# The expert router fed from the rows ahead of LayerNorm, in column halves

## The chip, the cores and the metric

The kernel runs on one core of a Trainium2 chip. The metric is device time in microseconds (us), as the median of several runs. TensorE does the matrix products, VectorE and ScalarE work on rows and on what TensorE leaves in PSUM, GpSimd builds constants and issues the gathers, SyncE issues nearly all loads. In the profile they are PE (PEld for its weight loads), DVE, ACT, POOL and SP; a q behind the name (SPq) is the engine's own queue of DMA issues and waits.

## The reference, cut to what matters

One layer on 512 tokens of 1024 channels, float32. Retention and a gated recurrence are projected, merged and passed through an output projection; then

```python
x = _layer_norm(DEEPNORM_ALPHA * x + merged @ w_out, ln1_g, ln1_b)
# hierarchical MoE
g_logits = xt @ w_group + b_group                    # 4 groups, argmax
e_logits = xt @ w_exp_router + b_exp_router          # 32 experts, top 2 inside the chosen group
h = silu(xb @ w_e_gate[e]) * (xb @ w_e_up[e]);  y = h @ w_e_down[e]
x = _layer_norm(DEEPNORM_ALPHA * x + moe, ln2_g, ln2_b)
```

Each of the 32 experts has three matrices of 2 MB, so 192 MB of weights are read, whatever the tokens choose.

## The kernel before

**Stages.** Everything up to the output projection works on channels by tokens, with every float32 operand split in a high and a low part and three products for each (`products`, L1367 to L1369). The output projection (`project`, L1543) gives rows: tile t of 128 tokens and column half `half` go into PSUM bank t, 8 blocks k of three products each. The order on TensorE is written out by hand: half 0 of tiles 0 to 3, then half 1 of tiles 0 to 3.

**LayerNorm 1 and the router.** For each of the eight half tiles VectorE waits for `proj_ok`, forms z = alpha * x + projection in place in `x2` (L1161) and takes the half's statistics (`half_stats`, L1138). After the second half of a tile, `layer_norm` (L1140 to L1153) aggregates them, has ScalarE take the root (L758), and writes the normalised tile over z in `x2` (`x2_ok`). TensorE then turns the whole tile into banks 4 and 5 with eight transposes (`turn_x2`, L1527), ScalarE copies it to `x2_t` (`x2t_out`, L733) and stores the tile to memory (`x2_dram`, L736), and TensorE multiplies it with the 36 router columns (`router`, L1535) into bank 6. The calls between the projections are: after `project(1, 1)` `turn_x2(0)`; after `project(1, 2)` `router(0)`, `turn_x2(1)`; after `project(1, 3)` `router(1)`, `turn_x2(2)`; then `router(2)`, `turn_x2(3)`, `router(3)`. VectorE adds the bias to all four tiles' logits at once and runs the selection: a chain of some twenty small operations up to `members_ok`, ranks by TensorE (L1584), `hot_r`, the lists by TensorE (L1593, L1598) and the row numbers `first_x` (L1253). GpSimd, which builds its constants once `proj_ok` has reached eight (L493), waits for `first_x` and for the stored rows, and gathers the rows of expert 0 from `x2_dram` (L511). In its waits TensorE runs products of the identity whose result is not used (`keep_warm`, 12, 3 and 14 calls).

**The experts.** SyncE loads the weights in pieces of 1 MB through a ring of 21 places (`load_m`, L412). Some places overlie older data and have a wait of their own:

```python
if n == 9:  sp.wait_ge(proj_ok, TT)
if n == 13: sp.wait_ge(proj_ok, 2 * TT)
if n == 19: sp.wait_ge(x2_ok, TT)
if n == 20: sp.wait_ge(routed, TT)
if n >= MRING: sp.wait_ge(m_done, n + 1 - MRING)
```

Piece 21 thus waits until the first half of expert 0's gate and up products has been used. For each expert TensorE turns the gathered rows (`turn_x`, L1608), multiplies with gate and up in two halves (`gate_up`, L1618), with down (L1647), and puts the result back to its tokens (`combine`, L1671). LayerNorm 2 and the output follow the last expert.

Of the kernel before, what the change touches and what calls it, by code (L numbers as in the profile page):

```python
# [48 lines left out]
OVER = (BLOCKS - 1) * EXPERTS  # L49
NO_ROW = 4096  # L50
NEAR = 4

# [78 lines left out]
def layer(nc, io, out):  # L131
    ctx = ExitStack()
    with ctx:
# [50 lines left out]
        x2 = at("x2", 64, [P, TT, D])  # L184
        x2_t = at("x2_t", 192, [P, 2, D])
        ln1_b_in, ln2_g_in = at("ln1_b_in", 196, [P, D]), at("ln2_g_in", 48, [P, D])
# [52 lines left out]
        hot_g, hot_1, hot_2, e8 = rt("hot_g", 16), rt("hot_1", 32), rt("hot_2", 32), rt("e8", 32)  # L239
        slot_i, red, res = rt("slot_i", 32, I32), rt("red", 4), rt("res", 64)  # L240
        assert rt_kb[0] <= 204.25
        ids, ids_w = at("ids", 128, [P, 2 * TT, 32]), at("ids_w", 129, [P, 2 * TT, 32])
# [34 lines left out]
        proj_ok, z_ok, x2_var, x2_std, x2_ok = (sem(n) for n in ("proj_ok", "z_ok", "x2_var", "x2_std", "x2_ok"))  # L277
        x2_turned, x2t_ok, routed, x2_stored = sem("x2_turned"), sem("x2t_ok"), sem("routed"), sem("x2_stored")
        router_in, consts_ok = sem("router_in"), sem("consts_ok")
# [33 lines left out]
        def _(sp):  # L313
# [66 lines left out]
            w_rt_v = w_rt[:, :].rearrange("p (k n) -> p k n", k=KD)  # L380
            for a in range(KD // NEAR):
                ks, rows_a = slice(NEAR * a, NEAR * a + NEAR), slice(P * NEAR * a, P * NEAR * (a + 1))
                sp.dma_start(w_rt_v[:, ks, 0:GROUPS], io["w_group"][0][rows_a].rearrange("(p b) n -> p b n", b=NEAR)).then_inc(router_in, 16)
                sp.dma_start(w_rt_v[:, ks, GROUPS:36], io["w_exp_router"][0][rows_a].rearrange("(p b) n -> p b n", b=NEAR)).then_inc(router_in, 16)
            sp.dma_start(b_rt[:, 0:GROUPS], row(io["b_group"])).then_inc(router_in, 16)
            sp.dma_start(b_rt[:, GROUPS:36], row(io["b_exp_router"])).then_inc(router_in, 16)
            load_qk(0, Unit(U_QK0))
            with sp.Fori(0, HEADS - 1) as h:
# [154 lines left out]
        def _(act):  # L543
# [188 lines left out]

            def x2t_out(t):  # L733

                act.wait_ge(x2_ok, t + 1)
                act.dma_start(x2_dram[t * P:(t + 1) * P, :], x2[:, t, :]).then_inc(x2_stored, 16)  # L736
                act.wait_ge(x2_turned, t + 1)
                if t >= 2:
                    act.wait_ge(routed, t - 1)
                if t == 0:  # L740
                    act.wait_ge(qk_split, 4 * HEADS)
                copy(x2_t[:, t % 2, :].rearrange("p (b n) -> p b n", b=2), bank[:, 4:6, :]).then_inc(x2t_ok, 1)

            def order_rows(dst, given):
# [8 lines left out]

            for t in range(TT):
                if t:
                    x2t_out(t - 1)
                act.wait_ge(x2_var, t + 1)
                act.activation(scale_v[:, 0:1], mv[:, 1:2], ACT.Sqrt).then_inc(x2_std, 1)  # L758
            x2t_out(TT - 1)

# [67 lines left out]
        def _(dve):  # L828
# [304 lines left out]
            dve.wait_ge(res_in, 16)  # L1133
            dve.wait_ge(ln1_ordered, 1)

# [3 lines left out]

            def layer_norm(t, ln, mid, start, end, var, std, ok):  # L1140
# [5 lines left out]
                z, g = (v.rearrange("q (c n) -> q c n", c=2) for v in (x2[:, t, :], ln[:, 0, :]))  # L1146
                step(dve.scalar_tensor_tensor(mid, z, mv[:, 0:1], g, ALU.subtract, ALU.mult))  # L1147
                dve.wait_ge(std, t + 1)
                step(dve.reciprocal(scale_v[:, 1:2], scale_v[:, 0:1]))
                step.wait()  # L1150
                for c_ in range(2):
                    cols = slice(512 * c_, 512 * c_ + 512)
                    last = dve.scalar_tensor_tensor(end(x2[:, t, cols]), start(mid[:, c_, :]), scale_v[:, 1:2], end(ln[:, 1, cols]), ALU.mult, ALU.add)  # L1153
                last.then_inc(ok, 1)

            for half in range(2):
                for t in range(TT):
                    n = TT * half + t + 1
                    dve.wait_ge(proj_ok, n)
                    z = x2[:, t, 512 * half:512 * half + 512]  # L1160
                    dve.scalar_tensor_tensor(z, z, ALPHA, bank[:, t, :], ALU.mult, ALU.add).then_inc(z_ok, 1)  # L1161
                    dve.wait_ge(z_ok, n)
                    half_stats(t, half)
                    if half:
                        mid = bank[:, t - 1:t + 1, :] if t else bank[:, 6:8, :]
                        layer_norm(t, ln1, mid, by_rows, stored_rows, x2_var, x2_std, x2_ok)


            dve.wait_ge(router_in, 96)
            dve.wait_ge(consts_ok, 1)  # L1170
            dve.wait_ge(routed, TT)
            lg = logit[:, :].rearrange("p (t n) -> p t n", t=TT)
            step(tt(lg, bank[:, 6, 0:TT * 36].rearrange("p (t n) -> p t n", t=TT),
                    b_rt[:, :].unsqueeze(1).to_broadcast([P, TT, 36]), ALU.add))
            step.wait()

# [176 lines left out]
            for t in range(TT):  # L1353
                half_stats(t, 0)
                half_stats(t, 1)
                mid = bank[:, 0:2, :] if t % 2 == 0 else bank[:, 4:6, :]
                layer_norm(t, ln2, mid, lambda v: v.rearrange("q (b p) -> q p b", b=NEAR),
                           lambda v: v.rearrange("q (p b) -> q p b", b=NEAR), f_var, f_std, f_ok)
# [3 lines left out]
        def _(pe):  # L1362
# [163 lines left out]

            def turn_x2(t):  # L1527
                pe.wait_ge(x2_ok, t + 1)
                if t:
                    pe.wait_ge(x2t_ok, t)  # L1530
                for k in range(KD):
                    last = pe.transpose(bank[:, 4 + k // 4, P * (k % 4):P * (k % 4) + P], x2[:, t, P * k:P * k + P], ident[:, :])
                last.then_inc(x2_turned, 1)

            def router(t):  # L1535
                pe.wait_ge(x2t_ok, t + 1)
                pe.wait_ge(router_in, 96)
                for k in range(KD):
                    last = pe.matmul(bank[:, 6, 36 * t:36 * t + 36], x2_t[:, t % 2, P * k:P * k + P], w_rt[:, 36 * k:36 * k + 36],  # L1539
                                     start=k == 0, stop=k == KD - 1)  # L1540
                last.then_inc(routed, 1)
# [16 lines left out]
            for t in (0, 1):  # L1558
                project(0, t, range(6, KD))
            for t in (2, 3):  # L1560
                project(0, t, range(KD))
            pe.wait_ge(ret_out, 8 * HEADS + 8)
            for t in range(TT):
                pe.wait_ge(z_ok, t + 1)
                project(1, t, range(KD))
                if t:
                    if t >= 2:
                        router(t - 2)
                    turn_x2(t - 1)
            router(TT - 2)  # L1570
            turn_x2(TT - 1)
            router(TT - 1)

            def keep_warm(n):

                for _ in range(n):
                    pe.matmul(bank[:, 1, 0:P], ident[:, :], ident[:, :], start=True, stop=True)

            keep_warm(12)
            pe.wait_ge(members_ok, 1)  # L1580
# [188 lines left out]
```

## Time and profile before

| what | us |
|---|---|
| median of 3 runs (lowest, highest) | 1299.18 (1298.66, 1301.23) |
| the profiled execution's own time | 1297.71 |
| its span | 1295.7 |
| what lies around the span | 2.0 |
| busy in the span: PE, DVE, ACT, POOL | 1246.7, 656.3, 410.8, 63.7 |

All times of rows are counted from the start of the span. A share of 1.0 in the DMA column means that all 16 DMA engines are busy; PEclk is the clock granted to TensorE as a share of 2.4 GHz, so 0.50 is 1.2 GHz. Durations of single matmuls overlap; the chain of waits gives how long they take in sequence.

### The profile page before, as it was taken

The numbers are of one execution on the slowest core, as the hardware profiler recorded it, in microseconds if no ns is written. First come the engines' busy times: TensorE is split into PE (matmuls) and PEld (weight loads), VectorE is DVE, ScalarE is ACT, GpSimd is POOL, SyncE is SP. The second block draws the span as 40 slices with busy tenths as digits, with TensorE's granted clock in tenths as the row PEclk, the third lists the DMA queues.
The fourth block names the chain that finished last, engine by engine and source line by source line (L and its number), as shares of the span: only waits on it lengthen the run. The fifth ranks groups of instructions, "written<-read, shape, count | busy, mean of one in ns | idle before, by whom it ended". The sixth has DMA issues, their size and how long they took to land.

```text
span 1295.7 us, 16051 instructions
## 1 busy us (share of the span) xinstructions
PE 1246.7 (96%) x6122; PEld 844.2 (65%) x6122; DVE 656.3 (51%) x946; ACT 410.8 (32%) x572; POOL 63.7 (5%) x70
## 2 busy tenths in 40 slices
PE   7999999999999999999999998999999999999892
PEld 6888887887888888888888887343343343334331
DVE  5496666335447337437433855244444444444347
ACT  4766755222433333333343412111111111111111
POOL 1000000000000000000005201000000000000000
PEclk9999999999999999999999998999999999999997
DMA  8322222363323223222223399799999999999992
GB/s 248 87 84 81 83 82 73 85 171 96 99 66 98 81 81 94 82 77 86 81 76 103 102 406 426 311 416 408 418 415 415 413 415 420 411 416 418 411 413 83
DMA packets 141512, 286.11 MB, mean 221 GB/s; under 512 B 9984, under 2 KB 107376, under 8 KB 116880
## 3 DMA queue, kind: packets, MB, share of 16 engines
q1 hardware_dynamic: 137680, 276.81, 57.2%
q0 software_dynamic: 2624, 4.33, 1.0%
q10 hardware_dynamic: 1152, 4.19, 0.9%
q8 instruction: 38, 0.62, 0.2%
q14 instruction: 18, 0.15, 0.0%
HBM read 285.17 MB, written 4.33 MB: 223 GB/s over the span
## 4 chain that ended last, share of the span: by engine, by line
PE 88%; DMA 7%; DVE 2%; ACT 1%; issue 1%; ACTq 0%; SPq 0%; DVEq 0%; POOLq 0%
PE bank L1367 19%; PE bank L1368 19%; PE bank L1369 19%; PE bank L1618 15%; PE bank L1647 7%; DMA m_raw<-in_w_e_up_dram 6%; PE bank L1671 4%; PE bank L1640 1%; PE bank L1608 1%; PE bank L1539 1%; PE bank L1467 1%; DMA x_rows<-in_x_dram 1%; DVE x L1153 0%; DVE stats L1138 0%; DVE bank L1147 0%
## 5 line engine op out<-in xcount | busy, mean ns | idle before, releaser
L836 DVE TENSOR_TENSOR w_lo<-raw,w_hi 128x1024 fp32r<-128x1024 f32 x120 | 148.4, 1238 | 184.8 <-ACT w_hi L545 183.5
L1618 PE MATMUL bank<-m_raw,xe 128*64 128x512 f32 x1024 | 233.4, 598 | 7.8 <-DMA m_raw<-in_w_e_up_dram 7.0
L832 DVE TENSOR_TENSOR x<-x,bank 128x1024 f32<-128x1024 f32 x124 | 145.8, 1217 | 170.9 <-PE bank L1671 170.9
L1367 PE MATMUL bank<-xt_hi,w_hi 128*128 128x512 f32 x576 | 225.0, 391 | 2.5 <-ACT merge L634 1.0
L1369 PE MATMUL bank<-xt_hi,w_lo 128*128 128x512 f32 x576 | 224.2, 389 | 0.0
L1368 PE MATMUL bank<-xt_lo,w_hi 128*128 128x512 f32 x576 | 224.1, 389 | 0.0
L545 ACT ACTIVATE w_hi<-raw 128x1024 fp32r<-128x1024 f32 x120 | 126.2, 1057 | 172.2 <-PE bank L1369 172.1
L1618 PEld LDWEIGHTS bank<-m_raw,xe 128*64 128x64 f32 x1024 | 70.2, 136 | 133.5 <-issue 132.5
L1367 PEld LDWEIGHTS bank<-xt_hi,w_hi 128*128 128x128 f32 x576 | 108.1, 188 | 25.8 <-ACT merge L634 1.4
L1369 PEld LDWEIGHTS bank<-xt_hi,w_lo 128*128 128x128 f32 x576 | 108.1, 188 | 22.6
L1368 PEld LDWEIGHTS bank<-xt_lo,w_hi 128*128 128x128 f32 x576 | 108.2, 188 | 21.9
L1647 PE MATMUL bank<-m_raw,ht 128*64 128x512 f32 x496 | 113.3, 598 | 0.0
L545 ACT ACTIVATE gu_sb<-bank 128x512 f32<-128x512 f32 x32 | 19.1, 598 | 258.8 <-PE bank L1618 258.8
L1647 PEld LDWEIGHTS bank<-m_raw,ht 128*64 128x64 f32 x496 | 32.9, 136 | 55.3 <-issue 53.3
L1307 DVE SCALAR_TENSOR_TENSOR y_lo<-bank,first_w,y_hi 128x512 fp32r<-128x512 f32 x31 | 23.3, 751 | 84.2 <-ACT y_hi L791 84.2
L1671 PEld LDWEIGHTS bank<-y_hi,pick 64*128 64x128 f32 x248 | 23.2, 184 | 55.0 <-issue 48.7
L1671 PE MATMUL bank<-y_hi,pick 64*128 64x512 f32 x248 | 55.5, 444 | 2.0 <-DVE y_lo_last L1307 1.6
L791 ACT ACTIVATE y_hi<-bank,first_w 128x512 fp32r<-128x512 f32 x31 | 21.3, 687 | 93.1 <-PE bank L1647 93.1
L511 POOL DMA_INDIRECT xg<-x_dram,first_x x32 | 30.1, 939 | 412.4 <-PE bank L1608 392.9
L1367 PE MATMUL bank<-w_hi,xt_hi 128*128 128x512 f32 x128 | 49.8, 389 | 0.0
L1367 PE MATMUL bank<-ret_hi,w_hi 128*128 128x512 f32 x128 | 49.8, 389 | 0.0
L1368 PE MATMUL bank<-w_lo,xt_hi 128*128 128x512 f32 x128 | 49.8, 389 | 0.0
(252 smaller groups left out, 1675.2 us busy)
## 6 DMA issues: line engine op xcount, KB each, us to landing
m_raw<-in_w_e_gate_dram SPq DMA_DIRECT2D x64, 1024.0 KB, 27.1
m_raw<-in_w_e_up_dram SPq DMA_DIRECT2D x64, 1024.0 KB, 26.5
m_raw<-in_w_e_down_dram SPq DMA_DIRECT2D x64, 1024.0 KB, 27.4
raw<-in_w_in_dram SPq DMA_DIRECT2D x88, 512.0 KB, 3.9
raw<-in_w_ret_o_dram SPq DMA_DIRECT2D x16, 512.0 KB, 3.3
raw<-in_w_lru_o_dram SPq DMA_DIRECT2D x16, 384.0 KB, 3.3
raw<-in_w_out_dram SPq DMA_DIRECT2D x8, 512.0 KB, 3.5
x_rows<-in_x_dram ACTq DMA_DIRECT2D x4, 512.0 KB, 5.4
```

The source lines that it names most:

```text
L511: pool.indirect_dma_start(xg[0:ROWS, :], None, x2_dram, bass.IndirectOffsetOnAxis(ap=idx, axis=0), bounds_check=last_x, oob_is_err=False). ...
L545: return act.activation(dst, src, ACT.Copy)
L791: act.activation(stored_rows(dst[:, :]), by_rows(bank[:, b, :]), ACT.Identity, scale=w).then_inc(yhi_ok, 1)
L832: return dve.tensor_tensor(dst, a, b, op)
L836: return dve.tensor_tensor(dst, a, b_r.bitcast(F32), ALU.subtract)
L1307: dve.scalar_tensor_tensor(stored_rows(dst[:, :]), by_rows(bank[:, b, :]), w, stored_rows(high[:, :].bitcast(F32)), ALU.mult, ALU.subtract ...
L1367: pe.matmul(dst, sh, mh, start=first and x == 0, stop=False)
L1368: pe.matmul(dst, sh, ml, start=False, stop=False)
L1369: ins = pe.matmul(dst, sl, mh, start=False, stop=last and x == n - 1)
L1618: last = pe.matmul(bank[side:side + ROWS, 0, :], xe[:, 4 * half + k, :], w[:, FE * k:FE * k + FE], start=half == 0 and k == 0, stop=half = ...
L1647: last = pe.matmul(bank[ROWS * c_:ROWS * c_ + ROWS, b, :], h[:, 2 * half + k, :], w[:, D * k + 512 * c_:D * k + 512 * c_ + 512], start=hal ...
L1671: last = pe.matmul(bank[:, (2 if t % 2 == 0 else 6) + b, :], choose[side:side + ROWS, P * t:P * t + P], y[side:side + ROWS, :], start=x == ...
```

## The change

The router's input is no longer the normalised tile but z. With LayerNorm written out, x . w = rstd * (z . (g w) - mean * sum(g w)) + sum(b w), and the mean is folded in as well by taking each column's mean off g w. So the router matrix is scaled by `ln1_g` and centred once, and only the factor rstd of a row and a constant row are left for the end.

- **Fold.** `w_rt` is loaded with channel k * 128 + p on partition p in place k (two DMAs instead of four), and `ln1_g` and `ln1_b` as 16 rows `ln_rows` (two more DMAs). TensorE turns these rows once (before tile 2 of half 0), VectorE forms g w and b w and their sums over k (`fold_ln`, after its second half tile), TensorE sums over partitions with a matrix of ones (after half 0), VectorE finishes matrix and bias (`fold_totals`, after its fourth half tile).
- **Half tiles.** The unit of turning and routing is a half tile: four transposes into bank 4 or 5 (`turn_z`), one copy of 128 x 512 (`zt_out`), four products (`router`). They run in the order `TURNS`, and TensorE's calls are put inside the projections of half 1: after blocks 0 and 1, and after blocks 2 to 4; the router calls stand behind the projection.
- **Logits.** The halves of tiles 0 to 2 that were routed in half 0 are copied out of bank 6 once and added later (`logits`); tile 3 accumulates in bank 7. `layer_norm` writes over z only once the half tile has been turned.
- **Store.** `store_x2` is a step of its own in ScalarE's order. `keep_warm(12)` becomes `keep_warm(16)` and writes bank 5.

```diff
+TURNS = (0, 1, 2, 4, 3, 5, 6, 7)
                 if n == 20:
-                    sp.wait_ge(routed, TT)
+                    sp.wait_ge(routed, 2 * TT)
...
+            def zt_out(n):
+                act.wait_ge(z_turned, n + 1)
+                if n >= 4:
+                    act.wait_ge(routed, n - 3)
+                if n == 0:
+                    act.wait_ge(qk_split, 4 * HEADS)
+                if n == 2:
+                    act.wait_ge(ln1_ordered, 1)
+                copy(z_t[:, n % 4, :], bank[:, 4 + n % 2, :]).then_inc(zt_ok, 1)
...
+            for n in range(3):
+                zt_out(n)
+            root(0)
+            zt_out(3)
+            zt_out(4)
+            store_x2(0)
+            root(1)
+            zt_out(5)
+            store_x2(1)
+            root(2)
+            zt_out(6)
+            store_x2(2)
+            zt_out(7)
+            root(3)
+            store_x2(TT - 1)
...
+            def fold_ln():
+                dve.wait_ge(router_in, 96)
+                step(dve.memset(ones[:, :], 1.0))
+                dve.wait_ge(ln_turned, 1)
+                step(tt(wb3, w3, bank[:, 7, KD:2 * KD].unsqueeze(2).to_broadcast([P, KD, 36]), ALU.mult))
+                step.wait()
+                step(tt(w3, w3, bank[:, 7, 0:KD].unsqueeze(2).to_broadcast([P, KD, 36]), ALU.mult))
+                step(dve.tensor_reduce(w_sum[:, 36:72], wb3.rearrange("p k n -> p n k"), AX, ALU.add))
+                step.wait()
+                dve.tensor_reduce(w_sum[:, 0:36], w3.rearrange("p k n -> p n k"), AX, ALU.add).then_inc(w_summed, 1)
+            def fold_totals():
+                dve.wait_ge(w_totals, 1)
+                step(tt(b_rt[:, :], b_rt[:, :], bank[:, 7, 100:136], ALU.add))
+                dve.scalar_tensor_tensor(w3, bank[:, 7, 64:100].unsqueeze(1).to_broadcast([P, KD, 36]), -1.0 / D, w3,
+                                         ALU.mult, ALU.add).then_inc(w_folded, 1)
+            def logits(t):
+                dve.wait_ge(routed, TURNS.index(TT + t) + 1)
+                base = b_rt[:, :]
+                if t < TT - 1:
+                    step(dve.scalar_tensor_tensor(lg[:, t, :], lg[:, t, :], rstd[:, t:t + 1], base, ALU.mult, ALU.add))
+                    step.wait()
+                    base = lg[:, t, :]
+                dst = bank[:, 7, 0:36] if t == TT - 1 else bank[:, 6, 36 * t:36 * t + 36]
+                dve.scalar_tensor_tensor(lg[:, t, :], dst, rstd[:, t:t + 1], base, ALU.mult, ALU.add).then_inc(logits_ok, 1)
             for half in range(2):
                 for t in range(TT):
                     n = TT * half + t + 1
+                    if n == 2 * TT:
+                        logits(0)
+                        logits(1)
...
+                    if n == 2:
+                        fold_ln()
+                    if n == TT:
+                        fold_totals()
+                    if n == TT + 1:
+                        dve.wait_ge(routed, 3)
+                        dve.tensor_copy(lg[:, 0:3, :], bank[:, 6, 0:108].rearrange("p (t n) -> p t n", t=3)).then_inc(halves_read, 1)
...
+            logits(2)
+            logits(3)
...
             for t in range(TT):
                 pe.wait_ge(z_ok, t + 1)
-                project(1, t, range(KD))
-                if t:
-                    if t >= 2:
-                        router(t - 2)
-                    turn_x2(t - 1)
-            router(TT - 2)
-            turn_x2(TT - 1)
-            router(TT - 1)
+                project(1, t, range(2))
+                turn_z((0, 3, 5, 6)[t])
+                if t == 0:
+                    turn_z(1)
+                project(1, t, range(2, 5))
+                if t < 2:
+                    turn_z((2, 4)[t])
+                project(1, t, range(5, KD))
+                for n in ((0, 1, 2), (3,), (4, 5), (6,))[t]:
+                    router(n)
+            turn_z(7)
+            router(7)
```

## Rows read from the trace of the kernel before

**Rows 1.** Groups of waits, 750 to 1296 us: us in total, times, longest.
```profile
PE bank L1618 <- DMA m_raw<-in_w_e_up_dram: 7.0, 10, 1.3
```
**Rows 2.** Chain that ended last, in order of time: start, us, what.
```profile
777.85 1.71 PE bank L1539 x16
779.56 0.91 PE bank L1532 x8
...
808.68 3.63 DMA xg<-x_dram,first_x
...
813.81 7.09 PE bank L1618 x32
...
1223.82 26.22 DMA m_raw<-in_w_e_up_dram
```
**Rows 3.** Stretches: busy us (count) of each engine, clock, DMA share, GB/s.
```profile
808.00:812.00 4.00, 3.85 (x47) 3.62 (x43) 3.11 (x17) 0.00 (x0) 1.03 (x1) 1.00 0.67 273
812.00:816.00 4.00, 2.87 (x18) 1.35 (x20) 1.86 (x6) 0.60 (x1) 1.00 (x1) 1.00 0.15 41
816.00:820.00 4.00, 4.00 (x22) 1.43 (x20) 0.00 (x0) 0.00 (x0) 0.00 (x0) 1.00 0.38 102
...
1200.00:1220.00 20.00, 17.28 (x92) 7.10 (x90) 7.26 (x9) 3.12 (x6) 0.94 (x1) 1.00 1.02 408
```
**Rows 4.** VectorE in order of time: start, us, line, operation, shapes [idle before].
```profile
760.68 0.69 DVE L1161 SCALAR_TENSOR_TENSOR x<-x,bank 128x512 f32<-128x512 f32 x1 [1.18 <-PE bank L1369]
...
785.98 0.69 DVE L1161 SCALAR_TENSOR_TENSOR x<-x,bank 128x512 f32<-128x512 f32 x1 [2.72 <-PE bank L1369]
...
789.74 0.16 DVE L1149 RECIPROCAL scale_v<-scale_v 128x1 f32<-128x1 f32 x1 [0.71 <-ACT scale_v L758]
789.94 1.41 DVE L1153 SCALAR_TENSOR_TENSOR x<-bank,scale_v,ln 128x512 f32<-128x512 f32 x2
...
798.52 0.17 DVE L1185 TENSOR_REDUCE res<-logit 128x4 f32<-128x16 f32 x1
...
803.44 0.29 DVE L832 TENSOR_TENSOR mem_bf<-mem 128x128 bf16<-128x128 f32 x1
```
**Rows 5.** SyncE's queue, issues of weight pieces 12, 13 and 20 (with 21).
```profile
761.99 0.81 SPq L423 DMA_DIRECT2D m_raw<-in_w_e_gate_dram  x1
785.97 0.33 SPq L423 DMA_DIRECT2D m_raw<-in_w_e_up_dram  x1
...
798.07 19.75 SPq L423 DMA_DIRECT2D m_raw<-in_w_e_down_dram  x2
```
**Rows 6.** DMA issues of six short stretches (762, 786, 798, 818, 808, 844): us to landing.
```profile
m_raw<-in_w_e_gate_dram SPq DMA_DIRECT2D x1, 1024.0 KB, 29.0
...
m_raw<-in_w_e_up_dram SPq DMA_DIRECT2D x1, 1024.0 KB, 7.4
...
m_raw<-in_w_e_down_dram SPq DMA_DIRECT2D x1, 1024.0 KB, 13.9
...
m_raw<-in_w_e_down_dram SPq DMA_DIRECT2D x1, 1024.0 KB, 4.8
...
xg<-x_dram,first_x POOLq DMA_INDIRECT x1, 3.6
...
xg<-x_dram,first_x POOLq DMA_INDIRECT x1, 7.2
```
**Rows 7.** TensorE in order of time, around the granted clock's low stretch.
```profile
789.67 1.98 PE L1539 MATMUL bank<-w_rt,x_t 128*128 128x36 f32 x16 [1.11 <-ACT x_t L545]
...
794.41 3.63 PE L1539 MATMUL bank<-w_rt,x_t 128*128 128x36 f32 x16 [1.11 <-ACT x_t L545]
797.84 4.84 PE L1577 MATMUL bank<-ident 128*128 128x128 f32 x24
...
808.46 3.39 PE L1577 MATMUL bank<-ident 128*128 128x128 f32 x28
812.44 0.68 PE L1608 MATMUL bank<-ident,xg 64*128 64x64 f32 x8 [0.59 <-DMA xg<-x_dram,first_x]
```
**Rows 8.** Stretches as in Rows 3, where the granted clock fell.
```profile
791.60:792.30 0.70, 0.70 (x6) 0.70 (x5) 0.00 (x0) 0.00 (x0) 0.00 (x0) 0.52 1.08 456
```

More of the change, by code:

```diff
@@ L184, in layer @@
         x2 = at("x2", 64, [P, TT, D])
-        x2_t = at("x2_t", 192, [P, 2, D])
+        z_t = at("z_t", 192, [P, 4, D // 2])
+        w_b, ones, w_sum = at("w_b", 192, [P, KD * 36]), at("ones", 193.125, [P, P]), at("w_sum", 193.625, [P, 72])
         ln1_b_in, ln2_g_in = at("ln1_b_in", 196, [P, D]), at("ln2_g_in", 48, [P, D])
@@ L240, in layer @@
         slot_i, red, res = rt("slot_i", 32, I32), rt("red", 4), rt("res", 64)
+        ln_rows, rstd = rt("ln_rows", P), rt("rstd", TT)
         assert rt_kb[0] <= 204.25
@@ L380, in _ @@
             w_rt_v = w_rt[:, :].rearrange("p (k n) -> p k n", k=KD)
[L381 to L384, printed above, removed]
+            sp.dma_start(w_rt_v[:, :, 0:GROUPS], io["w_group"][0].rearrange("(k p) n -> p k n", p=P)).then_inc(router_in, 16)
+            sp.dma_start(w_rt_v[:, :, GROUPS:36], io["w_exp_router"][0].rearrange("(k p) n -> p k n", p=P)).then_inc(router_in, 16)
             sp.dma_start(b_rt[:, 0:GROUPS], row(io["b_group"])).then_inc(router_in, 16)
             sp.dma_start(b_rt[:, GROUPS:36], row(io["b_exp_router"])).then_inc(router_in, 16)
+            for r, name in ((0, "ln1_g"), (KD, "ln1_b")):
+                sp.dma_start(ln_rows[r:r + KD, :], io[name][0].rearrange("(k p) -> k p", p=P)).then_inc(router_in, 16)
             load_qk(0, Unit(U_QK0))
@@ L752, in _, with store_x2, root @@
             order_rows(ln1[:, 1, :], ln1_b_in).then_inc(ln1_ordered, 1)
-            for t in range(TT):
-                if t:
-                    x2t_out(t - 1)
+            def store_x2(t):
+                act.wait_ge(x2_ok, t + 1)
+                act.dma_start(x2_dram[t * P:(t + 1) * P, :], x2[:, t, :]).then_inc(x2_stored, 16)
+            def zt_out(n):
[7 more added lines that the diff above has]
+                copy(z_t[:, n % 4, :], bank[:, 4 + n % 2, :]).then_inc(zt_ok, 1)
+            def root(t):
                 act.wait_ge(x2_var, t + 1)
                 act.activation(scale_v[:, 0:1], mv[:, 1:2], ACT.Sqrt).then_inc(x2_std, 1)
-            x2t_out(TT - 1)
+            for n in range(3):
[13 more added lines that the diff above has]
+            store_x2(TT - 1)
             act.wait_ge(exp_ok, 1)
@@ L1133, in _, with layer_norm @@
             dve.wait_ge(res_in, 16)
-            dve.wait_ge(ln1_ordered, 1)
             def half_stats(t, half):
                 step(dve.bn_stats(stats[:, 12 * t + 6 * half:12 * t + 6 * half + 6], x2[:, t, 512 * half:512 * half + 512]))
-            def layer_norm(t, ln, mid, start, end, var, std, ok):
+            def layer_norm(t, ln, mid, start, end, var, std, ok, inv=scale_v[:, 1:2]):
                 step.wait()
@@ L1148, in layer_norm @@
                 dve.wait_ge(std, t + 1)
-                step(dve.reciprocal(scale_v[:, 1:2], scale_v[:, 0:1]))
+                step(dve.reciprocal(inv, scale_v[:, 0:1]))
                 step.wait()
+                if ln is ln1:
+                    dve.wait_ge(z_turned, TURNS.index(TT + t) + 1)
                 for c_ in range(2):
                     cols = slice(512 * c_, 512 * c_ + 512)
-                    last = dve.scalar_tensor_tensor(end(x2[:, t, cols]), start(mid[:, c_, :]), scale_v[:, 1:2], end(ln[:, 1, cols]), ALU.mult, ALU.add)
+                    m = mid[c_][:, 0, :] if len(mid) == 2 else mid[0][:, c_, :]
+                    last = dve.scalar_tensor_tensor(end(x2[:, t, cols]), start(m), inv, end(ln[:, 1, cols]), ALU.mult, ALU.add)
@@ L1524, in _, with turn_z, router @@
             pe_ret(HEADS - 1, Unit(U_RET3))
[L1527 to L1540, printed above, removed]
+            def turn_z(n):
+                t, half = TURNS[n] % TT, TURNS[n] // TT
+                pe.wait_ge(z_ok, TURNS[n] + 1)
+                if n >= 2:
+                    pe.wait_ge(zt_ok, n - 1)
+                for k in range(4):
+                    last = pe.transpose(bank[:, 4 + n % 2, P * k:P * k + P], x2[:, t, 512 * half + P * k:512 * half + P * k + P], ident[:, :])
+                last.then_inc(z_turned, 1)
+            def router(n):
+                t, half = TURNS[n] % TT, TURNS[n] // TT
+                pe.wait_ge(zt_ok, n + 1)
+                if n == 0:
+                    pe.wait_ge(w_folded, 1)
+                if TURNS[n] == TT:
+                    pe.wait_ge(halves_read, 1)
+                if TURNS[n] == TT - 1:
+                    pe.wait_ge(x2_ok, 1)
+                if TURNS[n] == 2 * TT - 2:
+                    pe.wait_ge(logits_ok, 2)
+                one = t == TT - 1
+                dst = bank[:, 7, 0:36] if one else bank[:, 6, 36 * t:36 * t + 36]
+                for k in range(4):
+                    last = pe.matmul(dst, z_t[:, n % 4, P * k:P * k + P], w_rt[:, 36 * (4 * half + k):36 * (4 * half + k) + 36],
+                                     start=k == 0 and not (one and half), stop=k == 3 and (half == 1 or not one))
                 last.then_inc(routed, 1)
@@ L1559, in _ @@
                 project(0, t, range(6, KD))
+            pe.wait_ge(ret_out, 8 * HEADS + 8)
+            pe.wait_ge(router_in, 96)
+            pe.transpose(bank[:, 7, 0:2 * KD], ln_rows[0:2 * KD, :], ident[0:2 * KD, 0:2 * KD]).then_inc(ln_turned, 1)
             for t in (2, 3):
                 project(0, t, range(KD))
[L1562 removed]
+            pe.wait_ge(w_summed, 1)
+            pe.matmul(bank[:, 7, 64:136], ones[:, :], w_sum[:, :], start=True, stop=True).then_inc(w_totals, 1)
             for t in range(TT):
                 pe.wait_ge(z_ok, t + 1)
[L1565 to L1572 removed]
+                project(1, t, range(2))
[10 more added lines that the diff above has]
+            router(7)
             def keep_warm(n):
                 for _ in range(n):
[L1577 to L1579 removed]
+                    pe.matmul(bank[:, 5, 0:P], ident[:, :], ident[:, :], start=True, stop=True)
+            keep_warm(16)
             pe.wait_ge(members_ok, 1)
```

35 lines of the change are left out of this document (15 added, 20 removed).

## The prediction

> **What bounds the kernel now.** The groups of waits come first, because they say which wait ends last. From 750 us on TensorE waits ten times for a weight load, 7.0 us in all [rows 1]; the chain of waits then ends in such loads, the last seen from 1223.82 to 1250.04 [rows 2], and in the stretches the DMA engines are full while TensorE is not (17.28 of 20 us at 1200) [rows 3]. So the end is set by the stream of 192 MB, and only DMA time that is lost ahead of it counts. The stretches show where it is lost: 808 to 820, with shares of 0.67, 0.15 and 0.38, that is 1.3 + 3.4 + 2.5 = 7.2 us [rows 3]. The ring of 21 pieces is full, and piece 21 has to wait for the first half of expert 0, issued with piece 20 in a pair of issues from 798.07 to 817.82 [rows 5]. Expert 0 starts at 813.81 and its first half takes half of 7.09 us [rows 2]. Hence the rule for this change: the end moves as the start of expert 0 moves, one to one, until the 7.2 us are used up. What leads to that start is LayerNorm, router, selection (798.52 to 808.68), gather (808.68 to 812.31), turning, copy [rows 2, 4].
>
> **The projection's second half gets longer.** It runs from 760.68 to 785.98, the starts of VectorE's fourth and eighth half tile [rows 4]. Inside it lie two turnings and one router tile. A turning of eight transposes takes 0.91 us in the chain, a router tile 1.71 [rows 2]. After the change seven half turnings and six half router tiles lie inside it: 3.5 x 0.91 + 3 x 1.71 against 2 x 0.91 + 1.71, so +4.8 us. The fold adds to its start: VectorE's memset, two products, two sums of 288 columns between its second and third half tile, about 2.1 us by operations of like size in the selection (0.4 to 0.5 each). It delays nothing but the sums that TensorE waits for after half 0; by my count they come at 760.3, just in time, and the product with ones costs 0.2 us. I charge 0.3 us. The last projection ends at 786.0 + 5.1 = 791.1; bounds 790.5 (parts overlap) to 792.3 (a half costs 0.1 us more than half a whole, and a stall of 0.5).
>
> **The tail behind it gets shorter.** Before: from 785.98 to 798.52, 12.5 us, with the second, third and fourth router tile behind the projection and TensorE at half clock for the last (3.63 us where a tile had taken 1.71) [rows 4, 7]. After: TensorE has only half tiles 6 and 7 left (0.85 + 0.46, a copy of 0.6 with its two hops, 0.85), done at about 794.3. So VectorE is late next. It runs from 785.98 to 791.35 for the last tile, of which 0.71 is a wait for the root [rows 4]; without it 4.7 us, then `logits(2)` and `logits(3)`, three operations on 36 columns with their waits, 0.7 us. 791.1 + 4.7 + 0.7 = 796.5, against 798.52: **-2.0 us** for the start of the selection, bounds -2.6 to -0.8. The root stands behind the last copy in ScalarE's order, at about 793.3; VectorE needs it at 794.3, so that is covered by a us. `logits(0)` and `logits(1)`, 0.8 us, lie in VectorE's wait for the last projection. GpSimd's constants now start at 791.1 and took 3.1 us; they are needed at 796.5. The last row store goes out at 796.0 and takes some 8 us: 804, ahead of the gather, and ScalarE's scaling behind it (3.9 us) is done before the copy for expert 0. SyncE's two more small loads at 275 us cost 0.9 us in a queue that is four pieces ahead. These edits cost nothing.
>
> **Piece 13 is late, and with it the ring.** Piece 13 waits for the last projection: issued at 785.97, now at 791.2 [rows 5]. Before, this cost nothing: piece 12, issued at 762, landed 29.0 us later, at 791.0, and piece 13 right behind it, at 793.4 [rows 6]. Now the queue is empty at 791.0. A piece sent into an empty queue takes 4.8 us, as the one issued after 817 did [rows 6], so piece 13 lands at 796.0, 2.6 us later, and all behind it too: piece 20 at 814.6 instead of 812.0 (798.07 + 13.9) [rows 5, 6]. That stays within the ring's idle time, so it costs nothing by itself. But the gather then meets full DMA engines.
>
> **The gather.** It goes out at 808.68 - 2.0 = 806.7. Before, the queue was running dry, and it landed in 3.6 us; with loads queued, as at 844, it takes 7.2 [rows 6]. At 806.7 there are now 7.9 us of weights ahead of it. 806.7 + 7.2 = 813.9, against 812.3 [rows 2]: **+1.6 us** at expert 0. Bounds: 3.6 us (810.3, -2.0) and 814.6 + 0.3, when all weights are in (+2.6). I take 7.2, by the row with the same load. The Trainium skill says (DMA: Bandwidth & Descriptors, Queues, rings and completion order) that each DMA engine goes round between the rings that have work, a packet at a time. Read as equal turns, 64 rows would hardly be held up, the gather would keep its 3.6 us, and the sum would be -2.0: the first rival. The trace does not agree with that reading: 7.2 us under load.
>
> **TensorE's clock.** Before, it fell to 1.2 GHz at 791.6 [rows 8], after a gap of 1.1 us and a router tile of short products [rows 7]. Then came 24 identity products in 4.84 us. The clock was back when 28 took 3.39 us, and those ended 0.59 us before the gathered rows [rows 7]. Now the 14 calls begin about 2 us earlier and end at 809.9, and the rows come at 813.9: a gap of 4.0 us. A second gap of some 4 us stands ahead of the ranks: `keep_warm(16)` starts at 794.3, runs 32/28 x 3.39 = 3.9 us at full clock, and `mem_bf` comes at 803.44 - 2.0. Gaps of that size are not in the rows at full clock; one of 1.1 us with short products was enough once. Cost: nothing if the clock stays. If it is low when expert 0 begins, its turning (0.70) and first half (3.55) take up to twice their time, +4.3 us at most. Low at the lists (L1593) would put the gather back by up to 1 us. I take 1.4 us, a third of the upper end, as the clock may come back midway. The Trainium skill's rule (TensorE: Matmul & The Clock Gate, The HAM clock gate) is that full clock has to be earned by activity and is lost in idle stretches; it speaks against this change, which moves idle time right ahead of the first expert, and taken by itself it gives the upper end, a sum of +5.9.
>
> **Sum.** -2.0 (selection earlier) + 3.6 (gather 7.2 instead of 3.6) + 1.4 (clock) = +3.0 us. The profiled execution, 1297.71 = 1295.7 + 2.0, would become 1300.7; it lay 1.5 below the median, and on the median I forecast 1299.18 + 3.0 = 1302.2 us.
>
> **The rivals.**
> - *The gather keeps its 3.6 us.* Then expert 0 starts 2.0 us earlier; 1297.2. For it: the first gather did take 3.6 us while DMA engines were still full for its first us. Against: it landed at 812.3, just when piece 20 did. More than 2.4 us can't be won this way: piece 20 lands at 814.6, and the first half of expert 0 ended at 817.4. This is the case on the other side, and it decides at a gather of 5.6 us: below that the kernel is faster.
> - *The clock is low from the ranks to the end of expert 0's first half.* +1.6 + 4.3 and up to 1 at the lists: some +5.5, 1304.7. For it: two new gaps. Against: `keep_warm` with products of 128 columns did bring the clock back.
> - *Clock high all along.* Only the gather: +1.6, 1300.8; I count it in the forecast's own case, as its lower part.
> - *The second half grows less than I say*, because half tiles fit between blocks at less than their price in the chain: the last projection at 789, piece 13 hardly late, everything 4 us earlier up to the gather: about -3, 1296.
>
> **Chances.** Forecast's case 0.56, own range 1300.3 to 1304.0; gather fast 0.24; clock low throughout 0.12; the last 0.08. A difference of 0.2%, 2.6 us, is about what a measurement can tell here. The forecast's case gives slower 0.34, same 0.21, faster 0.01; the fast gather same 0.14, faster 0.10; the low clock slower 0.12; the last faster 0.05, same 0.02, slower 0.01. Together slower 0.47, same 0.37, faster 0.16. The range 1296.3 to 1305.0 holds the three first cases nearly whole.
>
> **What would show it.** The eighth half tile at 791 on VectorE; the selection's first reduction at 796.5; the issue of piece 13 at 791, and a stretch just after with a DMA share clearly below 1; the first gather issued near 807, landing after 7 us; TensorE idle for some 4 us before the first turning, and the clock of that stretch; piece 21 issued at 819 or later. I am wrong if the gather lands in under 5.6 us, or if the last projection ends before 789.5.

## The result and the profile after

The kernel after the change takes 1303.34 us (median of 10 runs, 1301.9 to 1304.94), the kernel before 1299.74 us on the same chip (10 runs, 1298.66 to 1301.54). The ratio is 1.0026, with a 95% interval of 1.0017 to 1.0035: 3.4 us slower, between 2.2 and 4.5. The forecast was 1302.2 us from a start of 1299.18, that is +3.0 us. The profiled execution took 1303.06 us with a span of 1301.4; before, these were 1297.71 and 1295.7. Two disturbed executions, the profiled one of e1 (1603 us at a granted clock of 0.75) and one of the kernel before (4467 us), are left out of the ratios and intervals.

The stage begins alike in both traces: the first weight piece is issued at 747.23 before and at 746.95 after. So times can be read side by side, to 0.3 us.

Stretches of the kernel after, columns as in [rows 3]:

```profile
784.00:788.00 4.00, 4.00 (x28) 3.56 (x28) 3.33 (x7) 0.78 (x2) 0.00 (x0) 1.00 0.95 397
788.00:792.00 4.00, 4.00 (x23) 3.40 (x21) 2.21 (x7) 0.03 (x1) 0.42 (x4) 1.00 0.36 147
792.00:796.00 4.00, 3.31 (x28) 3.00 (x28) 3.86 (x8) 0.69 (x2) 2.66 (x8) 1.00 0.88 305
...
804.00:808.00 4.00, 3.22 (x61) 3.25 (x62) 1.25 (x4) 2.75 (x3) 0.22 (x1) 0.50 1.02 428
808.00:812.00 4.00, 4.00 (x32) 3.94 (x31) 3.24 (x17) 1.15 (x2) 0.81 (x1) 0.70 1.01 427
812.00:816.00 4.00, 1.38 (x15) 1.08 (x13) 1.69 (x6) 0.12 (x1) 0.00 (x0) 1.00 0.84 324
816.00:820.00 4.00, 3.47 (x10) 1.07 (x12) 0.00 (x0) 0.48 (x1) 0.96 (x1) 0.65 0.13 39
820.00:824.00 4.00, 4.00 (x20) 1.39 (x18) 0.00 (x0) 0.00 (x0) 0.00 (x0) 0.92 0.28 51
```

Read the last but one column first, the DMA share. It has a new hole at 788 to 796 (0.36 and 0.88), where the queue waits for piece 13. Where [rows 3] had 0.67, 0.15, 0.38 from 808 to 820 there now stand 1.01, 0.84, 0.13, and the hole goes on to 824. Then the clock column: 0.50 at 804, and low a second time from 816 on.

VectorE in order of time, after, against [rows 4]:

```profile
761.10 0.67 DVE L1228 SCALAR_TENSOR_TENSOR x<-x,bank 128x512 f32<-128x512 f32 x1
...
791.54 0.69 DVE L1228 SCALAR_TENSOR_TENSOR x<-x,bank 128x512 f32<-128x512 f32 x1 [1.72 <-PE bank L1442]
...
794.50 0.16 DVE L1176 RECIPROCAL rstd<-scale_v 128x1 f32<-128x1 f32 x1
...
796.82 0.17 DVE L1258 TENSOR_REDUCE res<-logit 128x4 f32<-128x16 f32 x1
```

The eighth half tile comes 5.6 us later than before, the selection's first reduction 1.7 us earlier (798.52 before). The reciprocal has lost its wait of 0.71 us for the root.

SyncE's queue after, against [rows 5]: pieces 13, 20 (with 21) and 22.

```profile
791.53 0.33 SPq L430 DMA_DIRECT2D m_raw<-in_w_e_up_dram  x1
...
796.50 25.73 SPq L430 DMA_DIRECT2D m_raw<-in_w_e_down_dram  x2
822.28 0.43 SPq L430 DMA_DIRECT2D m_raw<-in_w_e_gate_dram  x1
```

The pair with piece 21 ends at 822.23, before at 817.82. From here on the text speaks of piece 22, the row of its own right behind that pair: 822.28 against 817.86, **+4.4 us**.

DMA issues of two short stretches after (791, 807), as in [rows 6]: us to landing in the last column.

```profile
m_raw<-in_w_e_up_dram SPq DMA_DIRECT2D x1, 1024.0 KB, 5.0
...
xg<-x_dram,first_x POOLq DMA_INDIRECT x1, 7.2
```

TensorE after, against [rows 7], from the lists to expert 0:

```profile
804.78 1.92 PE L1687 MATMUL bank<-ids,hot_r 128*64 128x32 f32 x32 [1.40 <-DVE hot_r L858]
806.47 1.93 PE L1692 MATMUL bank<-ids_w,hot_r 128*64 128x32 f32 x32
808.34 4.36 PE L1671 MATMUL bank<-ident 128*128 128x128 f32 x28
815.16 0.68 PE L1702 MATMUL bank<-ident,xg 64*128 64x64 f32 x8 [2.47 <-DMA xg<-x_dram,first_x]
816.53 8.78 PE L1712 MATMUL bank<-m_raw,xe 128*64 128x512 f32 x32 [0.69 <-ACT xe L552]
```

Before, the lists took 1.13 us each and the 32 products of expert 0's first pass 7.09. At the other end the time is still set by loads, as the groups of waits show against [rows 1]; the chain's last wait for a load now ends at 1255.81 instead of 1250.04.

```profile
PE bank L1712 <- DMA m_raw<-in_w_e_up_dram: 8.1, 12, 1.6
```

**Theory.** The time moves one to one with the DMA time that is lost ahead of the continuous stream. It can be read from the stretches: the sum over eleven stretches of 4 us from 784 to 828 of 4 x (1 - share) is 6.8 us before and 10.2 after, +3.4 us, which is what the runs show. Two causes lie under it: the gather meets a queue that is still full because piece 13 was late, and TensorE's clock falls. Rivals: the hole at piece 13 costs by itself; the clock does it all; the gather is slow for a reason of its own.

### The profile page after: what moved, and what is told of

Same layout as the page of the kernel before. It is cut to its first block, busy times and chain, and to the rows that moved or that the text cites. A ratio compares the mean times of both kernels' runs of the same rounds, so it can differ in the third digit from the quotient of the medians.

```text
span 1301.4 us, 16103 instructions
## 1 busy us (share of the span) xinstructions
PE 1247.4 (96%) x6133; PEld 843.6 (65%) x6133; DVE 660.2 (51%) x961; ACT 411.7 (32%) x576; POOL 63.8 (5%) x70
## 4 chain that ended last, share of the span: by engine, by line
PE 87%; DMA 7%; DVE 3%; ACT 1%; SPq 1%; issue 1%; DVEq 0%; ACTq 0%; POOLq 0%
PE bank L1440 19%; PE bank L1441 19%; PE bank L1442 19%; PE bank L1712 15%; PE bank L1741 7%; DMA m_raw<-in_w_e_up_dram 6%; PE bank L1765 4%; PE bank L1734 1%; PE bank L1702 1%; DMA xg<-x_dram,first_x 1%; PE bank L1540 1%; SPq L430 1%; DVE x L1183 0%; DVE stats L1163 0%; DMA vec_rows<-in_b_merge_dram 0%
## 5 line engine op out<-in xcount | busy, mean ns | idle before, releaser
L1442 PE MATMUL bank<-w_hi,xt_lo 128*128 128x512 f32 x128 | 49.8, 389 | 0.0
```

The lines of the kernel that those rows point to most:

```text
L1442: ins = pe.matmul(dst, sl, mh, start=False, stop=last and x == n - 1)
```

## The experiments

Each was timed beside the kernel before, on the same chip. "Lost" is the sum just described, from the experiment's own trace; "piece 22" is its issue, in the trace's own time. In e6, e9 and e11 the first weight piece goes out at 747.92, 748.06 and 747.90, 0.7 to 0.8 us later than in before, and piece 22 has to be read with that.

| run | piece 22 | lost, us | ratio [95%] | in us |
|---|---|---|---|---|
| before | 817.86 | 6.8 | | |
| after | 822.28 | 10.2 | 1.0026 [1.0017, 1.0035] | +3.4 |
| e1_warm (trace: e11) | 820.70 | 7.4 | 1.0013 [1.0004, 1.0022] | +1.7 |
| e2_late13 | 821.85 | 10.6 | 1.0026 [1.0015, 1.0037] | +3.4 |
| e3_late13_warm | 821.68 | 9.6 | 1.0039 [1.0026, 1.0051] | +5.1 |
| e4_hold18 | 818.53 | 7.6 | 1.0007 [0.9997, 1.0016] | +0.9 |
| e5_late_expert | 821.38 | 10.4 | 1.0030 [1.0018, 1.0042] | +3.9 |
| e6_routers_behind | 824.37 | 11.1 | 1.0025 [1.0015, 1.0036] | +3.3 |
| e7_hold19 | 815.76 | 3.9 | 0.9983 [0.9974, 0.9993] | -2.2 |
| e8_hold20 | 820.40 | 7.9 | 1.0006 [0.9995, 1.0016] | +0.8 |
| e9_before_hold20 | 818.85 | 6.6 | 0.9994 [0.9983, 1.0005] | -0.8 |
| e10_hold19_cold | 816.71 | 4.6 | 0.9975 [0.9963, 0.9986] | -3.3 |
| e12_root_first | 815.77 | 4.0 | 0.9995 [0.9984, 1.0005] | -0.6 |

### The stream's rule by itself: a late expert

```diff
 # before
-keep_warm(14)
+keep_warm(30)
```

> The kernel before with only 30 calls of identity products instead of 14 ahead of expert 0: they end near 815.7, 3.3 us after the gathered rows are there. Loads, gather and clock are as before. Theory A (the end moves one to one with the end of expert 0's first half, by DMA time lost with a full ring): +3.3 us, the gather still 3.6 us. Rival B (only the empty queue at 788 to 794 costs): 0. Rival D (TensorE had time to spare behind it, as it waits for loads at the end anyway): 0 to +1.

TensorE's identity products now outlast the gather, and nothing else is touched. The gather landed in 3.2 us, expert 0 started at 817.33 (before 813.81), piece 22 came at 821.38, both +3.5. Stretches of this run:

```profile
808.00:812.00 4.00, 4.00 (x64) 3.96 (x62) 2.85 (x18) 0.00 (x0) 1.03 (x1) 1.00 0.71 284
812.00:816.00 4.00, 4.00 (x37) 3.88 (x37) 2.41 (x7) 0.00 (x0) 0.00 (x0) 1.00 0.00 0
816.00:820.00 4.00, 3.31 (x23) 1.47 (x24) 0.00 (x0) 0.60 (x1) 0.96 (x1) 1.00 0.13 37
```

The share of 0.00 is the price: 10.4 us lost against 6.8, +3.6, and the runs say +3.9 (+2.3 by the medians, 1302.63 against 1300.32). A late start of expert 0 costs its own length, with no late piece and no slow gather.

### The late piece 13 alone

```diff
 # before
-if n == 13: sp.wait_ge(proj_ok, 2 * TT)
+if n == 13: sp.wait_ge(x2_ok, TT)
 # e3 also
-keep_warm(14)
+keep_warm(30)
```

> The kernel before with one edit: piece 13 waits for the last LayerNorm tile (791.4) instead of the last projection (786.0). Nothing of the router changes. Theory A: the load queue is still full when the gather goes out at 808.7, the gather takes 7.2 us instead of 3.6, expert 0 starts 3.6 us late, plus 0 to 4 us where the clock falls in the gap of 4 us ahead of it: +3.6 to +7 us. Rival B: +2.7 to +3.3 us, the empty queue's time, whatever the gather does. Rival C (the ring's idle time absorbs a late piece, and the gather does not depend on the loads): 0.

> As the kernel before with piece 13 waiting for the last LayerNorm tile, and 30 calls of identity products instead of 14 ahead of expert 0, which keep TensorE's clock. Theory A: the gather alone, +3.6 us (3.2 to 4.0); the difference to the run without the 30 calls is the clock's share. Rival B: +2.7 to +3.3. Rival C: the gather takes 3.6 us, but the products end at 815.7, so +3.3 by them.

The wait for the normalised tiles puts piece 13 where the change puts it: issued at 790.78 in e2, in the old kernel. This makes the whole slowdown: +3.4 us. The time alone does not tell theory A from rival B (+2.7 to +3.3); e4 below does. And e2 mixes both causes: its lists ran at half clock (1.92 and 1.93 us) and its gather took 6.1 us. In e3 the clock is full in the lists and in expert 0:

```profile
806.26 1.13 PE L1593 MATMUL bank<-ids,hot_r 128*64 128x32 f32 x32 [1.41 <-DVE hot_r L832]
807.19 1.13 PE L1598 MATMUL bank<-ids_w,hot_r 128*64 128x32 f32 x32
817.63 7.09 PE L1618 MATMUL bank<-m_raw,xe 128*64 128x512 f32 x32 [0.69 <-ACT xe L545]
```

Its gather, issued at 808.47, took 7.7 us, and piece 22 came 3.8 us later than before. So the gather is slow under load without any help from the clock.

The difference between the two runs was to be the clock's share. It came out the other way: e3 took +5.1 us (3.4 to 6.6) and e2 +3.4 (1.9 to 4.8), so these two runs give no share. Their traces say why little could be saved: the gather of e2, issued at 810.17, landed at 816.3 and that of e3, issued 1.7 us earlier, at 816.2. That e3 took more than its own piece 22 says is not explained.

### TensorE kept busy after the change

```diff
 # after
-keep_warm(16)
+keep_warm(30)
 ...
-keep_warm(14)
+keep_warm(30)
```

> The changed kernel with both long waits of TensorE filled: 30 calls of identity products instead of 16 ahead of the ranks, 30 instead of 14 ahead of expert 0. Theory A (the end moves one to one with the end of expert 0's first half; of the 4.4 us that this was late, about 2.6 come from the low clock: 0.8 at the lists, 1.7 in the first half): the lists take 1.13 us each, the gather goes out near 806.9 and still takes 7.2 us, expert 0's 32 products take 7.1 us, piece 22 goes out near 819.7, and the time is +1.0 to +2.0 us over the kernel before. Rival B (what costs is the 3.3 us of empty load queue between 788 and 794 by itself): +3.6 us, as the changed kernel.

> The changed kernel with 30 and 30 calls of identity products once more, for its trace: the lists at 1.13 us each, the gather near 806.9 with 7.2 us, expert 0's first 32 products in 7.1 us, piece 22 out near 819.7, and some 7.5 us of DMA time lost between 786 and 826.

The times are those of e1, the trace is that of e11, the same kernel. It is 1.7 us slower than before (0.5 to 2.9), where the change itself is 3.4 us slower (2.2 to 4.5): by these two numbers the clock is about half of the loss, but the intervals meet, so the share is known only roughly. In the trace of e11 the lists took 1.12 and 1.13 us, the first 32 products 7.09, and the gather 7.2 us. What is left, +1.7, is the forecast's case "clock high all along", +1.6. That single execution took 1303.62 us, though, with only 7.4 us lost, and from 1228 to 1258 the DMA engines moved 393 GB/s where the traces of all other kernels have 421 to 423. Its trace can be read for the start of the stage, not for the total.

### The same loads, held back from the gather

```diff
 # after
+if n == 18: sp.wait_ge(xg_in, 16)     # e4: first gather landed
```

> The changed kernel with one more wait: pieces 18, 19 and 20 are issued only when the first gather has landed. Theory A (the gather is slow because weight loads are queued; loads behind it can be made up in the ring's idle time): the queue is dry from about 807, the gather issued at 807.8 lands in 3.3 to 3.8 us instead of 7.2, expert 0 starts near 813.1, TensorE's gap ahead of it is closed; pieces 18 to 20 are in by 821, the stream's start of piece 21 is set by that: +1 to +2.5 us over the kernel before, 1 to 2.5 less than the changed kernel. Rival B (every us of empty queue before piece 21 costs a us): more empty queue ahead of the gather, so slower than the changed kernel, +5 us or more. Rival E (the gather is slow for a reason of its own, such as the later row store): it still takes 7 us and the time is +7 us.

Issued at 808.20, the gather took 3.8 us instead of 7.2. The issue of the gather, SyncE's queue and two stretches of e4:

```profile
xg<-x_dram,first_x POOLq DMA_INDIRECT x1, 3.8
```

```profile
811.99 0.33 SPq L432 DMA_DIRECT2D m_raw<-in_w_e_gate_dram  x1
812.36 0.43 SPq L432 DMA_DIRECT2D m_raw<-in_w_e_up_dram  x1
812.84 5.65 SPq L432 DMA_DIRECT2D m_raw<-in_w_e_down_dram  x2
818.53 0.43 SPq L432 DMA_DIRECT2D m_raw<-in_w_e_gate_dram  x1
```

```profile
808.00:812.00 4.00, 4.00 (x36) 3.94 (x35) 2.82 (x17) 1.55 (x2) 1.03 (x1) 0.64 0.14 40
812.00:816.00 4.00, 3.31 (x27) 2.17 (x27) 2.11 (x6) 0.60 (x1) 0.96 (x1) 1.00 0.78 254
```

Piece 13 was late here as well, the DMA engines were empty for most of four more us, and the lists were again at half clock. Still the kernel is 2.5 us faster than the change. A hole is no loss by itself: what counts is the sum of all of them, 7.6 us here, and this one is repaid because expert 0 starts at 814.48 instead of 816.53 and its first 32 products take 7.09 us instead of 8.78. That settles the rivals "the hole costs by itself" and "the gather is slow for a reason of its own": the row stores and the gather itself are those of the changed kernel.

### Router half tiles later, and a smaller hold

```diff
 # e6, on after: router calls behind project(1, t)
-for n in ((0, 1, 2), (3,), (4, 5), (6,))[t]:
+for n in ((0, 1, 2), (3,), (), (4, 5, 6))[t]:
 # (logits(1) moves behind the last tile's LayerNorm)
 # e7 and e8, on e6: keep_warm(25) and (16) for (16) and (14);
 # xg_in also awaited at n == 19 (e7) or at n == 20 (e8)
```

> The changed kernel with the router calls 4 and 5 (tile 3's first half, tile 1's second) moved behind the last projection, and the logits of tile 1 formed at the end. TensorE then has 5 us of work behind the last projection, as VectorE has. The last projection ends at 789.7 instead of 791.5, the selection starts near 795.5 instead of 796.8, the gather goes out 1.3 us earlier and still meets full DMA engines (7.2 us); the clock's fall stays. Theory A: 1.0 to 1.5 us less than the changed kernel, +2.3 us over the kernel before. Rival F (the length of the projection's second half is hidden by the ring): no difference to the changed kernel, +3.6.

> All of it together: router calls 4 and 5 behind the last projection, 25 and 16 calls of identity products where they fill TensorE's two waits, and pieces 19 and 20 held until the first gather has landed. Theory A: selection from 795.5, gather out at 805.7 and in 3.6 us, expert 0 from about 810.8, pieces 19 and 20 in by 816.7, so that the DMA engines are idle for 5 to 6 us in all instead of 7.2: 1 to 2 us less than the kernel before. Rival B (idle queue time is what counts, in the same amount): the same, -1 to -2, so this run does not tell A from B; it tests the version. If the gather is slow for a reason of its own: +4 us.

> As the version with pieces 19 and 20 held, but only piece 20 is held. The queue then runs dry at about 810, the gather lands with it at 810.6 to 811, one or two us later than with two pieces held, and one piece less has to be made up: 1.5 to 2.5 us less than the kernel before, by theory A. If the gather lands late (7.2 us, 813), 0 to -0.5.

e6 missed. The last projection did end earlier, by 0.8 us in the trace's time and 1.8 relative to the first weight piece, which is issued at 747.92 here. But VectorE gave most of that back, as it now waits for the root and has two more operations on logits ahead of the selection, which starts only 0.5 us earlier counted from the first weight piece:

```profile
790.74 0.69 DVE L1227 SCALAR_TENSOR_TENSOR x<-x,bank 128x512 f32<-128x512 f32 x1 [0.92 <-PE bank L1443]
...
794.53 0.16 DVE L1176 RECIPROCAL rstd<-scale_v 128x1 f32<-128x1 f32 x1 [0.74 <-ACT scale_v L769]
...
797.31 0.17 DVE L1259 TENSOR_REDUCE res<-logit 128x4 f32<-128x16 f32 x1
```

Its gather took 7.6 us, and its clock fell as after the change, for longer at expert 0 (some 10.0 us for the first 32 products): no gain, +3.3.

e7 is the first kernel that is faster than both before and after, by 2.2 us against before. The gather was issued at 806.68, the lists ran at full clock, and four stretches show where the time is not lost any more:

```profile
804.00:808.00 4.00, 3.52 (x77) 3.52 (x78) 2.27 (x10) 3.58 (x4) 1.03 (x1) 1.00 1.01 428
808.00:812.00 4.00, 3.27 (x31) 2.88 (x31) 3.65 (x17) 0.60 (x1) 0.70 (x1) 1.00 0.40 85
812.00:816.00 4.00, 4.00 (x20) 1.30 (x18) 0.00 (x0) 0.00 (x0) 0.41 (x1) 1.00 0.95 393
816.00:820.00 4.00, 3.81 (x26) 1.71 (x23) 0.10 (x1) 0.89 (x2) 0.06 (x1) 1.00 1.03 389
```

The held pieces, issued at 810.22 and 810.59, fill 812 to 816, and piece 21 follows by 815.71, so the DMA share stays near 1. The long hole of [rows 3] is gone. e7 differs from e6 in the hold and in the identity products; e10 below takes the second away.

e8 holds one piece less and missed its expected gain: +0.8. Piece 19 is still queued when the gather goes out at 806.75, the gather takes 6.4 us, TensorE waits 2.91 us for it, and its clock is low in the first 32 products:

```profile
813.16 7.19 SPq L432 DMA_DIRECT2D m_raw<-in_w_e_down_dram  x2
820.40 0.43 SPq L432 DMA_DIRECT2D m_raw<-in_w_e_gate_dram  x1
```

```profile
813.28 0.68 PE L1705 MATMUL bank<-ident,xg 64*128 64x64 f32 x8 [2.91 <-DMA xg<-x_dram,first_x]
814.65 8.79 PE L1715 MATMUL bank<-m_raw,xe 128*64 128x512 f32 x32 [0.69 <-ACT xe L554]
```

One piece of 1 MB more in the queue cost 2.9 us of gather and 4.6 us of piece 22, part of it through the clock.

### Is the hold enough without the change, and without the extra products?

```diff
 # e9, on before
+if n == 20: sp.wait_ge(xg_in, 16)
 # e10, on e7
-keep_warm(25) ... keep_warm(16)
+keep_warm(16) ... keep_warm(14)
 # e12, on e10, ScalarE's order
-zt_out(7)
 root(3)
+zt_out(7)
```

> The kernel before with piece 20 held until the first gather has landed; the router is as it was. Theory (the end moves as the DMA time that is lost before piece 21): the gather goes out at 808.7 and lands at 812 as before, since the queue runs dry at 809.6; piece 20 is sent at 812.3 and in at 817, about when piece 21 is released, so nothing is lost or won: 0 to +0.7 us. If so, the gain of the version with pieces 19 and 20 held comes from the earlier selection and not from holding loads alone. Rival G (holding loads is what made that version fast): -2 us.

> The version with pieces 19 and 20 held, with 16 and 14 calls of identity products as in the changed kernel instead of 25 and 16. Theory: the wait for the members leaves TensorE idle for 3 us, the clock falls in part of the executions, the lists then take 1.9 us each and the gather goes out 0.8 us later; the pieces held go out later by as much, and the products ahead of expert 0 end late by 1 to 2 us: +0.8 to +2 us over that version, -1.4 to 0 against the kernel before. Rival H (the clock costs nothing where DMA time is the limit): -2.2, as that version.

> The version with pieces 19 and 20 held and 16 and 14 calls of identity products, with ScalarE's root of the last tile ahead of the copy of the last half tile (it stood behind it, and VectorE waited 0.74 us for it in the run with the router calls behind the projection). Theory: VectorE's wait goes, the selection starts 0.7 us earlier, gather, held pieces and expert 0 too, the DMA time lost between 786 and 826 falls from 4.6 to about 4 us: 0.5 to 1 us less than that version, -3 to -4 us against the kernel before. Rival: the last copy then ends later (0.2 us) and its logits become the last to arrive, so only 0.2 us are won.

e9: the old kernel's gather fell from 3.6 to 2.8 us, and the time by 0.8 us, which its interval (2.2 less to 0.7 more) tells neither from nothing nor from rival G's -2. With one piece held, then, the changed router (e8, +0.8) is not ahead of the old one. That the gain of e7 and e10 needs the earlier selection is argued, not shown: the run that would tell, the kernel before with pieces 19 and 20 held, was not made.

e10 missed: I expected it 0.8 to 2 us above e7, and it is not slower (0.9975 against 0.9983, intervals overlap). Its lists ran at 1.64 and 1.97 us and its expert 0 began at 812.66, 0.95 later than in e7, but the first 32 products took their 7.09 us:

```profile
804.43 1.64 PE L1690 MATMUL bank<-ids,hot_r 128*64 128x32 f32 x32 [1.41 <-DVE hot_r L860]
805.80 1.97 PE L1695 MATMUL bank<-ids_w,hot_r 128*64 128x32 f32 x32
812.66 7.09 PE L1715 MATMUL bank<-m_raw,xe 128*64 128x512 f32 x32 [0.69 <-ACT xe L554]
```

TensorE went straight from its identity products to the gathered rows: here a short gather guarded the clock with no extra products.

e12 did what its edit says: no wait for the root, the selection at 795.75, expert 0 at 811.72, 4.0 us lost. I expected 3 to 4 us below before and measured 0.6, with bounds of 2.1 below and 0.7 above. By the rule it should have stood at -2.8. Its trace is of one of its best executions: 1297.28 us, the second fastest of 12 and 1.8 us below their median, and as fast as the traced ones of e7 (1296.84) and e10 (1297.39). Five of the 12 had a mean clock of 0.991 and took 1298.0 us in the mean; the slowest had 0.988 and 1302.03 us. So the trace doesn't show what the slower ones lost. e7, e10 and e12 were also timed on three different chips; whether the gain of e7 and e10 is partly chance is open.

## Why the prediction was right

The forecast of +3.0 us met +3.4 (ratio) and +3.6 (medians). Step by step:

- **What bounds the kernel.** Right: the end moves about one to one with the start of expert 0. Isolated by e5, 3.5 us for +3.9 (2.3 to 5.5). The runs give it a handier form: the sum of the holes in the DMA share up to 828 gives the times of the kernels, with a scatter of about 2 us.
- **The projection's second half.** 791.54 against 791.1 forecast. Counted from its first product on TensorE (760.48 before, 760.77 after) it grew by 5.3 us, where 4.8 were forecast. The fold lay on VectorE from 757.60 to 759.86, and TensorE did not wait for it; it began half 1 0.3 us later, as charged.
- **The tail.** 796.82 against 796.5. -1.7 us instead of -2.0: the projection ended 0.4 us later than forecast and the rest took 0.1 us less. The covers held: the reciprocal didn't wait for the root.
- **Piece 13.** Issued at 791.53 and landed in 5.0 us, at 796.5; forecast 791.2, 4.8 and 796.0. That it costs nothing by itself is what e4 shows.
- **The gather.** 7.2 us, as taken from the gather at 844. This term, +3.6, is the largest of the sum and it was right. e3 shows it without the clock (7.7 us), e4 and e7 take it away (3.8 and 3.5). Piece 20 was forecast in at 814.6 and landed at 816.9; the gather landed before it, at 815.0, so this did no harm.
- **The reading of the Trainium skill** (DMA: Bandwidth & Descriptors, Queues, rings and completion order) **as equal turns**, my rival on the faster side, fell: 6.1 to 7.7 us in after, e2, e3, e6, e8 and e11, where much was queued, 2.8 to 4.2 us where the queue was running dry or held. Nothing here shows in what order the packets were served.
- **The clock was the mis-sized term.** I charged 1.4 us in all and held a fall at the lists (up to 1 us) and one at expert 0 for the upper end. Both came. The lists took 1.92 and 1.93 us instead of 1.13 twice; as the second begins while the first runs, the gather went out 0.8 us late. The first 32 products took 8.78 us instead of 7.09. That is 2.5 us. The gap ahead of the ranks was 3.74 us, as forecast (4); that before expert 0 was 2.47 and not 4.0, because the identity products started later and at half clock. (The rival with the low clock all through was added up wrongly: +1.6, +4.3 and up to 1 are 5.9 to 6.9 us, not some 5.5.)

So in the profiled pair the sum is -1.7 + 3.6 + 0.8 + 1.7 = +4.4 us, the shift of piece 22, where the forecast had +3.0. The lost DMA time says +3.4, the runs +3.4 to +3.6. The profiled times differ by more, 5.35 us, since the profiled execution of before lay 2.0 us below its median and that of after 0.3 below. The interval of the runs, 2.2 to 4.5 us, holds both counts, so they don't decide between them.

The result was nearer than its terms, and that was luck: they were short by 1.1 us for the clock and 0.3 for the tail, and one count of the loss is a us above what many runs show.

## What to carry to other kernels

Where a stream of loads sets the end, sum 4 x (1 - DMA share) over the stretches ahead of it, for both kernels: the difference is an estimate of the price of a change (here good to 2 us), and a hole costs nothing if a later one shrinks by as much. A small gather on which the next stage waits should not be sent behind bulk loads that nobody needs yet. Hold those loads until it has landed: here three pieces held, and nothing else, brought the change from +3.4 to +0.9 us (e4). With two held and two router calls moved, it gained 2.2 and 3.3 us in two variants and 0.6, within the noise, in a third; with one held it gained nothing (e8).

## What the runs showed that I had not expected

- The gather of 64 rows took about as long as the weight loads that were issued before it still needed, up to some 7.5 us. From its issue to the landing of the last of them, and to its own: 3.3 and 3.6 us (before), 2.9 and 3.2 (e5), 3.1 and 3.5 (e7), 3.6 and 4.2 (e12), 6.0 and 6.1 (e2), 6.5 and 6.4 (e8), then 8.4 and 7.7 (e3), 9.1 and 7.2 (after), 10.2 and 7.2 (e11). With 0.9 us of loads left it still took 2.8 (e9). So what it costs can be read from the queue at its issue, and a gather that goes out earlier into the same queue need not land earlier.
- The same 32 products of expert 0 took 7.09 us in ten traces and 8.78, 8.79 and some 10.0 in after, e8 and e6. TensorE had waited for the gathered rows 2.47, 2.91 and 3.37 us in these three, and at most 1.17 us in the ten. In these three the slow gather was paid twice.
- At the lists there is no such order. They ran at half clock after a wait of 3.74 us ahead of the ranks (after), but also after 0.78 (e2), and at full clock after 1.59 (e5). What decides there is open.
- The 35 runs of the kernel before beside e6 to e8 spread from 1297.3 to 1302.9 us. The mean granted clock goes with it: the seven at 0.985 or below took 1301.9 us in the mean, the nine at 0.989 or above 1298.9. The traced execution of before had 0.989 and took 1297.71. One profile's span can't decide a difference of 3 us; the stretches up to 828 were the better measure.
